# The layer norm of the first half's values on ScalarE instead of VectorE, with two more convolution taps per channel block on VectorE

## The reference

```
A:  a, g, z = split(rmsnorm(x) @ w_in, 3)
    c  = a * sigmoid(g)
    y  = causal depthwise conv of c, 31 taps per channel, + bias
    x1 = x + rmsnorm((silu(layernorm(y)) * silu(z)) @ w_out)
B:  u, v = gelu(rmsnorm(x1) @ w_uv);  z = rmsnorm(x1) @ w_z        # 2048 channels each
    v  = layernorm(v)                       # over the 2048 channels of a frame
    s  = u * (W_s[group] @ v + b[group])    # in chunks of 128 frames, 8 groups of 256 channels
    y_out = x1 + rmsnorm((s * silu(z)) @ w_out)
```

## Time and profile before

| | us |
|---|---|
| median of 3 runs (lowest, highest) | 2373.88 (2373.14, 2373.99) |
| the profiled execution: its own time | 2372.43 |
| the profiled execution: span in the trace | 2370.6 |
| PE busy | 2305.1 (97%) |
| PEld busy | 2007.5 (85%) |
| DVE busy | 1583.9 (67%) |
| ACT busy | 795.7 (34%) |
| POOL busy | 244.3 (10%) |
| mean granted TensorE clock | 0.992 |

### The profile page before, as it was taken

How to read it: one execution, slowest core, us unless ns; L and a number is a source line. 1 busy time by engine, 2 the same in 40 slices (tenths; PEclk the granted TensorE clock), 3 DMA queues, 4 the chain that set the end, 5 groups by cost and what they waited for, 6 DMA issues and landing times.

```text
span 2370.6 us, 29559 instructions
## 1 busy us (share of the span) xinstructions
PE 2305.1 (97%) x12208; PEld 2007.5 (85%) x12208; DVE 1583.9 (67%) x1638; ACT 795.7 (34%) x1201; POOL 244.3 (10%) x419
## 2 busy tenths in 40 slices
PE   7899999999999998999989999999999998999998
PEld 6788899999888887888877878879999997888885
DVE  5599999987678888999955852276767676222221
ACT  5322223223442212222333542116665666111110
POOL 1100000011221110000000211111101000100000
PEclk9999999999999999999999999999999999999999
DMA  4323234332553222333443442213333336232220
GB/s 167 125 92 98 98 126 144 102 126 86 174 178 129 104 73 91 99 99 109 129 157 105 148 156 91 82 47 90 97 97 102 92 107 250 107 107 98 80 93 23
DMA packets 118438, 265.18 MB, mean 112 GB/s; under 512 B 16288, under 2 KB 52384, under 8 KB 116256
## 3 DMA queue, kind: packets, MB, share of 16 engines
q1 hardware_dynamic: 94816, 184.64, 24.1%
q0 software_dynamic: 23488, 78.64, 9.7%
HBM read 184.86 MB, written 78.75 MB: 111 GB/s over the span
## 4 chain that ended last, share of the span: by engine, by line
PE 91%; DVE 5%; DMA 2%; issue 1%; ACT 1%; POOL 0%; SPq 0%; DVEq 0%; ACTq 0%
PE PS L1834 29%; PE PS L1835 29%; PE PS L1836 29%; DVE acc L1337 2%; PE PS L2066 1%; PE PS L2038 1%; PE PS L1880 1%; PE PS L1902 1%; PE PS L1845 1%; DMA raw<-wa_in_in 0%; DVE Ul L1301 0%; DMA zb<-silu_z_scratch 0%; PE PS L1889 0%; DVE m L1555 0%; DMA xt<-x_in 0%
## 5 line engine op out<-in xcount | busy, mean ns | idle before, releaser
L1337 DVE SCALAR_TENSOR_TENSOR acc<-cp,cw,acc 128x1024 f32<-128x1024 f32 (+1 forms) x480 | 639.4, 1332 | 12.6
L1834 PE MATMUL PS<-HAh,Wh 128*128 128x512 f32 (+2 forms) x960 | 341.8, 356 | 0.4 <-DVE HAl L1301 0.4
L1835 PE MATMUL PS<-HAl,Wh 128*128 128x512 f32 (+2 forms) x960 | 340.0, 354 | 0.0
L1836 PE MATMUL PS<-HAh,Wl 128*128 128x512 f32 (+2 forms) x960 | 339.7, 354 | 0.0
L1834 PE MATMUL PS<-Wbh,s7h 128*128 128x512 f32 (+1 forms) x544 | 212.8, 391 | 8.0 <-issue 6.4
L1834 PE MATMUL PS<-Vh,HBh 128*128 128x512 f32 (+1 forms) x544 | 212.6, 391 | 1.8 <-DVE Vl L1301 1.7
L1835 PE MATMUL PS<-Wbl,s7h 128*128 128x512 f32 (+1 forms) x544 | 212.6, 391 | 0.0
L1836 PE MATMUL PS<-Wbh,s7l 128*128 128x512 f32 (+1 forms) x544 | 212.4, 391 | 0.0
L1835 PE MATMUL PS<-Vl,HBh 128*128 128x512 f32 (+1 forms) x544 | 212.0, 390 | 0.0
L1836 PE MATMUL PS<-Vh,HBl 128*128 128x512 f32 (+1 forms) x544 | 211.8, 389 | 0.0
L1834 PE MATMUL PS<-HBh,Uh 128*128 128x512 f32 x512 | 203.3, 397 | 0.8 <-ACT vb L1085 0.8
(11 more groups left out here) (215 smaller groups left out, 4601.9 us busy)
## 6 DMA issues: line engine op xcount, KB each, us to landing
raw<-wa_in_in SPq DMA_DIRECT2D x48, 512.0 KB, 3.6
rawv<-wb_v_in SPq DMA_DIRECT2D x64, 256.0 KB, 4.7
rawu<-wb_uz_in SPq DMA_DIRECT2D x32, 512.0 KB, 3.6
v_scratch<-vb POOLq DMA_DIRECT2D x64, 256.0 KB, 2.6
vt<-v_scratch SPq DMA_DIRECT2D x32, 512.0 KB, 4.1
s_scratch<-m POOLq DMA_DIRECT2D x32, 512.0 KB, 4.1
st<-s_scratch SPq DMA_DIRECT2D x16, 1024.0 KB, 4.9
xt<-x_in SPq DMA_DIRECT2D x16, 512.0 KB, 5.1
```

The lines of the kernel that those rows point to most:

```text
L1337: ins = nc.vector.scalar_tensor_tensor(out=a, in0=c[:, k:k + w], scalar=cw[:, j, k:k + 1], in1=a, op0=ALU.mult, op1=ALU.add)
L1834: nc.tensor.matmul(out, wh, xh, start=start, stop=False, skip_group_check=seeded)
L1835: nc.tensor.matmul(out, wh, xl, start=False, stop=False, skip_group_check=seeded)
L1836: return nc.tensor.matmul(out, wl, xh, start=False, stop=stop, skip_group_check=seeded)
```

## The change

`v_norm` of half 0 leaves DVE. In its place ACT runs eight Identity activations per block j, one for each tile of 128 frames, `vt = vrs * vt + vneg`, at the start of its own iteration j, before the Gelu of unit 2j. `vneg` = -mean * vrs (128x8) is made once by one DVE instruction ahead of the stage, for which DVE waits for `v_rs`. `u_vn` is now signalled by the last of the eight activations. Half 1 keeps its norm on DVE (`v_norm(j)`, the same instructions as before). In `tap_plan` the rooms of a U block grow from 3, 4, 4 to 4, 5, 4. No DMA, no matmul and no tile that existed before is changed.

```diff
@@ -57,7 +57,7 @@
 
     room = [(("A", n), 3 if n < 6 else 4 if n >= 44 else 7) for n in range(4, 2 * UNITS_A - 2)]
     room += [(("V", q, i), 2 if q == 0 or i % 2 == 0 else 3) for q in range(NQ) for i in range(8)]
-    room += [(("U", j, part), n) for j in range(KB) for part, n in enumerate((3, 4, 4))]
+    room += [(("U", j, part), n) for j in range(KB) for part, n in enumerate((4, 5, 4))]
     taps, ends, k = {}, {}, 0
     for key, n in room:
         hi = min(k + n, NBLK * TAPS)
@@ -126,6 +126,7 @@
         vbs = g("vbs", [P, len(TILES[1]), NQ, 6])
         vmv = g("vmv", [P, NTILES, 2])
         vrs = g("vrs", [P, NTILES])
+        vneg = g("vneg", [P, len(TILES[0])])
 
 
         r1_at = g.at
@@ -316,7 +317,7 @@
             ("sq", "eps", "r", "sc", "tr", "hi", "lo"))
         v_hi, v_lo, v_mm, v_gel, v_bn = (sem(f"v_{n}") for n in ("hi", "lo", "mm", "gel", "bn"))
         v_st = [sem(f"v_st{i}") for i in range(5)]
-        v_zero, v_agg, v_eps, v_rs = (sem(f"v_{n}") for n in ("zero", "agg", "eps", "rs"))
+        v_zero, v_agg, v_eps, v_rs, v_neg = (sem(f"v_{n}") for n in ("zero", "agg", "eps", "rs", "neg"))
         u_raw = [sem(f"u_raw{i}") for i in range(3)]
         u_hi, u_lo, u_mm, u_gel, u_silu, u_mu, u_mz = (sem(f"u_{n}") for n in
             ("hi", "lo", "mm", "gel", "silu", "mu", "mz"))
@@ -1084,8 +1085,18 @@
                             act.wait_ge(v_st[u % 5], 16 * (u // 5))
                         nc.scalar.activation(vb[u % 5][0:m, :], PS[0:m, v_bank(h, q, i), :], ACT.Gelu).then_inc(v_gel, 1)
 
+            def v_norm(j):
+
+                act.wait_ge(u_ldv, 16 * (j + 1))
+                act.wait_ge(v_neg, 1)
+                for i in range(8):
+                    b = vt[:, i, :]
+                    last = nc.scalar.activation(b, b, ACT.Identity, scale=vrs[:, i:i + 1], bias=vneg[:, i:i + 1])
+                last.then_inc(u_vn, 1)
+
             def u_stage():
                 for j in range(KB):
+                    v_norm(j)
                     for m in range(2):
                         n = 2 * j + m
                         to = (gu[0], sz)[m]
@@ -1496,31 +1507,27 @@
                     m = rows(t)
                     nc.vector.bn_aggr(vmv[0:m, t, :], vbs[0:m, i, :, :]).then_inc(v_agg, 1)
 
-            def v_norm(h, j):
-                first = TILES[h][0]
-                parts = ((P, slice(0, 8), slice(first, first + 8), 8),)
-                if h == 1:
-                    parts += ((N_SAMPLE, slice(8, 9), slice(16, 17), 1),)
-                count = KB * h + (h + 1) * (j + 1)
-                dve.wait_ge(u_ldv, 16 * count)
+            def v_norm(j):
+
+                parts = ((P, slice(0, 8), slice(8, 16), 8), (N_SAMPLE, slice(8, 9), slice(16, 17), 1))
+                dve.wait_ge(u_ldv, 16 * (KB + 2 * (j + 1)))
                 if j == 0:
-                    dve.wait_ge(v_rs, h + 1)
+                    dve.wait_ge(v_rs, 2)
                 for n, ts, of, k in parts:
                     b = vt[0:n, ts, :]
                     nc.vector.tensor_tensor(b, b, vmv[0:n, of, 0:1].to_broadcast([n, k, P]), ALU.subtract).then_inc(u_sub, 1)
-                dve.wait_ge(u_sub, count)
+                dve.wait_ge(u_sub, 2 * (j + 1))
                 for n, ts, of, k in parts:
                     b = vt[0:n, ts, :]
                     nc.vector.tensor_tensor(b, b, vrs[0:n, of].unsqueeze(2).to_broadcast([n, k, P]), ALU.mult)\
                         .then_inc(u_vn, 1)
-                if h == 1:
-                    dve.wait_ge(u_vn, count)
-                    dve.wait_ge(u_gb, 32 * (j + 1))
-                    if j >= 1:
-                        dve.wait_ge(u_vst, 16 * j)
-                    nc.vector.tensor_tensor(vo[:, :], vt[0:N_SAMPLE, 8, :], gb[:, 0, :], ALU.mult).then_inc(u_vom, 1)
-                    dve.wait_ge(u_vom, j + 1)
-                    nc.vector.tensor_tensor(vo[:, :], vo[:, :], gb[:, 1, :], ALU.add).then_inc(u_vo, 1)
+                dve.wait_ge(u_vn, KB + 2 * (j + 1))
+                dve.wait_ge(u_gb, 32 * (j + 1))
+                if j >= 1:
+                    dve.wait_ge(u_vst, 16 * j)
+                nc.vector.tensor_tensor(vo[:, :], vt[0:N_SAMPLE, 8, :], gb[:, 0, :], ALU.mult).then_inc(u_vom, 1)
+                dve.wait_ge(u_vom, j + 1)
+                nc.vector.tensor_tensor(vo[:, :], vo[:, :], gb[:, 1, :], ALU.add).then_inc(u_vo, 1)
 
             def u_add_bias(h, j):
                 if j == 0 and h == 0:
@@ -1561,7 +1568,6 @@
                     if j >= 1:
                         u_gate(j - 1, 1)
                     fill(("U", j, 0))
-                    v_norm(0, j)
                     if n + 2 < 2 * KB:
                         u_low(n + 2)
                     u_add_bias(0, j)
@@ -1750,7 +1756,7 @@
                         q_gate_u(1, j - 1)
                         q_gate_z(j - 1)
                     add_22(2 * j)
-                    v_norm(1, j)
+                    v_norm(j)
                     u_add_bias(1, j)
                     if j + 1 < KB:
                         q_add_up("T3", j + 1)
@@ -1801,6 +1807,9 @@
             for i in range(len(TILES[0])):
                 o_step(0, i)
             v_stage(0)
+            dve.wait_ge(v_rs, 1)
+            nc.vector.scalar_tensor_tensor(out=vneg[:, :], in0=vmv[:, 0:8, 0], scalar=-1.0, in1=vrs[:, 0:8], op0=ALU.mult,
+                                           op1=ALU.mult).then_inc(v_neg, 1)
             dve.wait_ge(u_ws, 16)
             nc.vector.memset(wst[P // 2:P, :, 0:P // 2], 0.0).then_inc(u_mask, 1)
             u_stage()
```

## The result

| | before | changed |
|---|---|---|
| median, us (lowest to highest) | 2373.93 (2373.14 to 2375.12), 4 runs | 2359.22 (2356.61 to 2360.28), 4 runs |
| ratio to before, 95% interval | | 0.9936 (0.9919 to 0.9953) |
| profiled execution: own time / span | 2372.43 / 2370.6 | 2358.49 / 2356.6 |
| mean granted clock | 0.992 | 0.995 |

The changed kernel is 14.7 us faster by the medians (forecast 13.4, to 2360.5; the range was 2357.5 to 2365.0).

What follows compares the result with a forecast made beforehand. PE, busy 97%, bounds the kernel, so gains come only where PE waits or DVE is on the chain. Savings of 6.4, 2.8, 1.1, 2.5 and 0.65 total 13.4 us: 2373.9 to 2360.5, range 2357.5 to 2365.0.

Steps and rivals of the forecast that it cites:

- Block 1: U stage of half 0: its mixing starts at 916.9 us, not 923.31, with the norm off DVE's path, saving 6.4 us.
- block 2: U stage: its mixing came 26.3 us after the one before, against PE's own 23.56; the slow clock's share, 2.8 us, goes.
- blocks 3 to 11: U stage: each falls from 23.68 us to PE's own 23.56, saving 1.1 us over the nine.
- block 12: U stage: 26.05 us becomes 23.56; the wait of 2.24 us before its mixing and its edge go, saving 2.5 us.
- block 13: Late U stage: PE's wait for the load of the convolution's last result goes, as taps end earlier, saving 0.65 us.
- rival 2: Late U stage: the 3.50 and 4.90 us waits or the clock behind them change: 2357 to 2359, or 2363 us; chance 0.12.
- The waits of 3.50 and 4.90 us stay: Late U stage: PE still waits for DVE's next-stage statistics; no gain taken, +/- 2 us kept for the range.
- the loop: Late U stage: PE waits for statistics behind low weights, which wait for ACT's copy after the Silu of PE's just-ended chunk.
- Two taps more cost nothing: U stage: DVE's block becomes 24.06 us against PE's 23.56; the margin shrinks from 6.7 to 2.2 us, without PE waits.
- Rival 1: U stage: DVE's block runs 0.25 us or more above 24.06, so PE waits: 2363.2 or 2366.8 us; chance 0.12.
- rival 4: U stage: ACT's reads and writes of `vt` slow DVE's taps; 2380.1 us at 26.5 us a DVE block; chance 0.03.
- Rival 3: U stage: ACT's norm lies on PE's path in each block, 0.8 us more each, 12.8 in all: 2386.7 us; chance 0.01.

## Why the prediction was right

**Block 1.** Forecast: the mixing at 916.9 and `vt` ready at 914.4. In order of time it is at 917.52, which is 916.9 less the late start, and ACT ends at 914.5, which is 913.9. The activations take 3.20 us for eight, the 3.18 of the Silu that I took as the nearest row.

**The terms of the sum**, by the mixings' places on the chain, the changed kernel's less 0.6:

| | forecast, us | measured, us |
|---|---|---|
| block 1: 923.31 against 917.08 | 6.4 | 6.2 |
| block 2: 949.64 against 940.64 | 2.8 | 2.8 |
| blocks 3 to 11 | 1.1 | 1.2 |
| block 12 | 2.5 | 2.4 |
| block 13: 1214.01 against 1200.24 | 0.65 | 1.2 |
| behind that, to the end of the span | 0 | 0.8 |
| sum | 13.4 | 14.6 |

The last two were sized too small. At block 13 not only the wait of 0.65 us went, but an edge beside it. Behind it, the time from block 14's mixing to block 15's is 31.70 us in place of 32.08, at a clock of 0.83 in the ten microseconds around the wait of 4.90 us, which had 0.66 before (1240 to 1250 us, against 1250 to 1260). This is rival 2's place, within the +/- 2 us kept for it. That looks like chance and not like the change: in the six other traces with this wait the same distance lies between 31.62 and 32.30 us, whichever engine has the norm. The remaining 0.4 us come behind block 15 and aren't explained. The profiled span is shorter by 14.0 us: these 14.6 less the late start.

The terms of blocks 1 and 2 are both there because the norm left DVE in block 2 as well: with block 1's alone moved, 3.5 of these 9 us came back as a wait in block 2.

**The waits of 3.50 and 4.90 us stay.** They did, and moving the statistics took both away: that the statistics stand behind the low weights is shown to be their cause, not only argued. The links of the loop in front of that, Silu, copy and low weights, are read from the rows.

**Two taps more cost nothing.** Forecast: DVE behind by 0.50 us a block, margin from 6.7 to 2.2 us; measured 0.5 and 2.1, and the experiment with one tap more found its end where the same sum had put it. Rival 1 and rival 4 had nothing for them: in the steady blocks DVE's instructions have the lengths of before. What hides the making of `vneg` was also as told: it takes 0.17 us behind a wait of 2.13 us for POOL's power, and DVE's wait for the mixing of block 0 is 4.12 us in place of 5.54.

**Rival 3.** The Trainium skill (ScalarE: Activation LUTs, Rules for kernel authors) has the rule that stood beside it: VectorE, not ScalarE, for adding and multiplying. On price the rule holds here, 3.20 us on ACT against 2.39 on DVE. The kernel is 14.7 us faster all the same, and with ACT's load raised by 3.5 us more in each block nearly as fast: the dearer engine had the time.

## What to carry to other kernels

Compare two engines by when the one's result is wanted, not by their busy shares: here DVE stayed at 98% (950 to 1140 us) and stopped costing anything, because the step that PE waits for left its queue. How late the fuller engine may run has to be counted block by block up to the last one: 13 taps were free and 14 were not. When a wait is taken away in one block alone, look for it in the next. A wait of 3.5 us that no load explains is worth a look at the order on the engine named: here one statistic behind one unrelated subtraction cost, twice, together with the clock, 12 us.

## What the runs showed of the hardware

- The clock after a wait: after waits of 6.24 and 7.01 us the next mixing ran at the lower of the two levels (16 rows in 3.78 and 3.79 us in place of 1.78 to 2.05), after one of 3.46 us it took 3.51. After waits of about 2.8 us it did so in some blocks and not in others: at 1112.73 and 1167.31 (2.83 us each) and, for most of it, at 1033.13 (2.81 us, 3.46), it did; at 980.44 (2.82 us) and 1086.06 (2.80 us) it didn't. After 2.27 us at 1188.80 in the kernel of block 1 alone it took 2.65 us (clock 0.83 from 1190 to 1200 us), after 2.24 us at the same place in the kernel before 2.05. So these traces give no length of wait that parts the two. The same 4.90 us wait is followed by a mean clock of 0.66 in one trace and 0.83 in another.
- A slower clock on PE reaches DVE, which has other work, only through others: Silu late, copy late, DVE idle (2.85 us in the kernel before, 0.44 and 1.80 with the taps alone, 1.20 with block 1 alone). So its cost isn't always hidden where DVE is the slower engine. Behind one of the slow mixings, at 1033.13, DVE didn't wait.
- Activations of 128x128 follow each other at 0.22 us if scale and bias are constants (Copy), and at 0.40 us if both are read per partition (Identity). The runs don't part the two operands from the change of function. The Trainium skill (ScalarE: Activation LUTs, What ACT_TABLE_LOAD costs) gives about 93 ns for each such operand; this trace agrees, with 0.18 us for the two.
